# GpSimd's scaling of the residual starts after the eighth remainder of a layer norm, and the rotary table's load goes ahead of it

## The reference, cut to what matters

```python
xp = _layer_norm(ALPHA * xp + yp, ln1_g[l], ln1_b[l])     # after the mixer
xp = _layer_norm(ALPHA * xp + fp, ln2_g[l], ln2_b[l])     # after the ConvFFN
# _layer_norm: (x - mean) * rsqrt(var + eps) * g + b
```

## Time and profile before

| | us |
|---|---|
| runs | 1981.17 median of 3 (1978.34 to 1981.82) |
| the profiled execution's own time | 1974.85 |
| its span | 1973.0 |
| PE busy | 1860.7 (94%) |
| DVE busy | 902.3 (46%) |
| ACT busy | 521.5 (26%) |
| POOL busy | 149.6 (8%) |

### The profile page before, as it was taken

One profiled execution on the slowest core, in us unless ns is written; L12 is line 12 of the kernel. 1 busy time (PEld: TensorE's weight loads), 2 busy tenths in 40 slices (PEclk: granted clock), 3 DMA queues, 4 the chain that ended last, 5 costly groups with the idle time before them and its releaser, 6 DMA issues.

```text
span 1973.0 us, 35556 instructions
## 1 busy us (share of the span) xinstructions
PE 1860.7 (94%) x13514; PEld 1615.0 (82%) x13514; DVE 902.3 (46%) x1442; ACT 521.5 (26%) x734; POOL 149.6 (8%) x119
## 2 busy tenths in 40 slices
PE   8897999997999999997999998998998799999996
PEld 8894555486999999996949948957966799999996
DVE  3635443436555255535245246236237655335544
ACT  3322222213222122214222222222222422222223
POOL 0200000001000000004111210300300200000000
PEclk9998999998999999999999999999999999999999
DMA  5437888711222222221323323234324123222221
GB/s 188 165 131 242 268 282 270 258 43 43 79 92 95 76 86 91 99 76 54 136 93 119 105 110 131 80 121 144 89 98 160 47 89 99 89 75 86 97 98 45
DMA packets 83912, 234.16 MB, mean 119 GB/s; under 512 B 9617, under 2 KB 9778, under 8 KB 83490
## 3 DMA queue, kind: packets, MB, share of 16 engines
q1 hardware_dynamic: 83138, 228.19, 35.1%
q0 software_dynamic: 736, 5.48, 0.8%
HBM read 209.84 MB, written 23.80 MB: 118 GB/s over the span
## 4 chain that ended last, share of the span: by engine, by line
PE 83%; DVE 5%; issue 2%; ACT 2%; DMA 1%; DVEq 0%; SPq 0%; ACTq 0%
PE banks L1169 62%; PE banks L1246 5%; PE banks L1445 2%; PE banks L1439 2%; PE banks L1359 2%; PE banks L1431 1%; PE banks L1277 1%; PE banks L1216 1%; PE banks L1268 1%; PE banks L1287 1%; PE banks L1419 1%; DVE x_lo L942 1%; DVE y L921 1%; DMA kv<-in_vc 1%; PE banks L1280 1%
## 5 line engine op out<-in xcount | busy, mean ns | idle before, releaser
L1169 PE MATMUL banks<-x_hi,w_hi 128*128 128x272 f32 x2624 | 548.9, 291 | 44.5 <-DVE x_lo L942 30.7
L1169 PE MATMUL banks<-x_hi,w_lo 128*128 128x272 f32 x2624 | 546.0, 290 | 0.0
L1169 PE MATMUL banks<-x_lo,w_hi 128*128 128x272 f32 x2624 | 544.3, 289 | 0.0
L620 DVE TENSOR_TENSOR w_lo<-w_raw,w_hi 128x1024 fp32r<-128x1024 f32 (+2 forms) x228 | 287.4, 1260 | 515.5 <-ACT w_hi L423 515.3
L423 ACT ACTIVATE w_hi<-w_raw 128x1024 fp32r<-128x1024 f32 (+2 forms) x228 | 238.4, 1046 | 1024.6 <-PE banks L1169 989.3
L1169 PEld LDWEIGHTS banks<-x_hi,w_hi 128*128 128x128 f32 x2624 | 415.6, 190 | 49.9 <-issue 28.4
L1169 PEld LDWEIGHTS banks<-x_lo,w_hi 128*128 128x128 f32 x2624 | 415.9, 190 | 0.0
L1169 PEld LDWEIGHTS banks<-x_hi,w_lo 128*128 128x128 f32 x2624 | 412.7, 190 | 0.0
L1169 PE MATMUL banks<-act_hi,w_lo 128*128 128x272 f32 x704 | 145.2, 287 | 0.0
L1169 PE MATMUL banks<-act_lo,w_hi 128*128 128x272 f32 x704 | 145.1, 287 | 0.0
L1169 PE MATMUL banks<-act_hi,w_hi 128*128 128x272 f32 x704 | 145.0, 287 | 0.0
(11 more groups left out here) (221 smaller groups left out, 1770.4 us busy)
## 6 DMA issues: line engine op xcount, KB each, us to landing
w_raw<-in_w_up SPq DMA_DIRECT2D x88, 512.0 KB, 3.5
kv<-in_kc SPq DMA_DIRECT2D x128, 256.0 KB, 4.3
kv<-in_vc SPq DMA_DIRECT2D x128, 256.0 KB, 3.8
w_raw<-in_w_rin SPq DMA_DIRECT2D x48, 512.0 KB, 3.5
w_raw<-in_w_dn SPq DMA_DIRECT2D x32, 704.0 KB, 4.1
s<-in_s SPq DMA_DIRECT2D x32, 512.0 KB, 7.4
out_ret_s<-s SPq DMA_DIRECT2D x32, 512.0 KB, 2.6
w_raw<-in_w_in_ab SPq DMA_DIRECT2D x20, 512.0 KB, 3.6
```

The lines of the kernel that those rows point to most:

```text
L620: V.tensor_tensor(w_lo[:, j, 0:k * P], w_raw[:, j, 0:k * P], w_hi[:, j, 0:k * P].bitcast(F32), ALU.subtract).then_inc(lo_ready, 1)
L1169: last = mm(B[:, 2 * j + half, 0:HN], a[:, j, w], x[:, kt, half * HN:(half + 1) * HN], start=kt == 0 and n == 0, stop=kt == k - 1 and n == 2)
```

## The change

In scale_residual GpSimd waits once for all eight remainders of the norm, and then issues its eight instructions without a wait between them. The load of the rotary table is issued as soon as norm 1's eighth remainder is there, ahead of the eight scalings; the memset of qm stays behind them.

```diff
             def scale_residual(n):
+                pool.wait_ge(ln_done, n * KD + KD)
                 for m in range(KD):
-
-                    pool.wait_ge(ln_done, n * KD + m + 1)
                     nc.gpsimd.tensor_scalar(y[:, m, :], y[:, m, :], lnp[:, n, 1, m:m + 1], ALPHA, ALU.add, ALU.mult)\
                         .then_inc(y_scaled, 1)
 
             scale_residual(0)
 
+            pool.wait_ge(ln_done, KD + KD)
+            pool.dma_start(rope[:, :, :], A["rope"]).then_inc(rope_in, 16)
             pool.wait_ge(y_scaled, 1 + KD)
             scale_residual(1)
-            pool.wait_ge(y_scaled, 1 + 2 * KD)
-            pool.dma_start(rope[:, :, :], A["rope"]).then_inc(rope_in, 16)
             nc.gpsimd.memset(qm[:, :, :, :], 0.0).then_inc(zeroed, 1)
             pool.wait_ge(rope_in, 16)
```

## The result

The changed kernel took 1967.25 us in the median of four executions (1964.35 to 1968.72), before took 1979.76 on the same occasion (1977.19 to 1981.82): ratio 0.9939, interval 0.9924 to 0.9954, which is 9 to 15 us faster. The forecast was 1975.0 in 1971.0 to 1980.5, a gain of 6.2. The profiled execution of the changed kernel has a span of 1965.4 us, 7.6 less than the one of before.

The account below looks back on a forecast made before the run. The prediction took TensorE to be bound by VectorE's x_lo in each norm's first tile, held by GpSimd. Norms 0, 1 and 2 gain 2.6 + 1.0 + 2.6 = 6.2 us; 1981.17 - 6.2 = 1975.0, range 1971.0 to 1980.5.

Parts of the forecast that it names:

- What bounds the kernel: First tile of each norm: TensorE waits for VectorE's x_lo, 30.7 us in 18 waits, held by GpSimd's scalings.
- The gain of a norm, 2.6 us: First tile of each norm: VectorE loses six delays, so TensorE takes the last slice 2.6 us earlier.
- The cost in norm 1, 1.6 us: Behind norm 1: w_lo of tile 2 stands behind the scaling, TensorE waits 1.6 us, norm 1 keeps 1.0 us.
- The cost in norms 0 and 2: Tile 2 behind these norms: scalings delay w_lo by up to 0.46 us, hidden because TensorE needs it later.
- The rope load: GpSimd's queue in norm 1: issued about 4 us earlier, nothing as an own term; its issue costs 0.57 us.
- The sum: Whole kernel: 2.6 + 1.0 + 2.6 = 6.2 us faster, 1975.0 us from the median 1981.17; chance 0.62.
- rival (a): TensorE's clock behind norm 0: the low stretch may not come, 1.5 us more gain, 1973.5; chance 0.13 in this sense.
- (b): Scalings behind the norms: 1.19 us each but VectorE gets in between; 2.3 us faster, 1978.9, or 1980.7 at 1.41; chance 0.13.
- (c): First tile of the norms: x_lo is held by something that stays, not GpSimd; 1982.6 us; chance 0.07.
- (d): Behind all three norms: queued scalings keep VectorE out, 1.41 us each; 9.6 us slower, 1990.8; chance 0.05.
- one resource used in turns: In each norm: VectorE's scale holds GpSimd's instruction until it ends, which then holds x_lo for about 0.46 us.

Follow-up runs that it names:

- e8: The kernel before with GpSimd's 24 scalings of norms 0, 1 and 2 left out; 10.1 us faster than before, ratio 0.9952.
- e3: The changed kernel with only norm 1 gathered, rope load ahead of its scaling, norms 0 and 2 as before; 1.4 us faster than before, ratio 0.9992.
- e12: The changed kernel with VectorE's two waits moved from the retention's head to where qm is written, run again; 9.2 us faster than before, ratio 0.9957.
- e16: Like e12, but GpSimd's scaling behind norm 1 begins only when the third tile's w_lo is done; 11.0 us faster than before, ratio 0.9942.

## Why the prediction was wrong, point by point

**What bounds the kernel.** Right: the largest wait of TensorE was the one that moved, 30.7 to 23.0 us. GpSimd as the one that held x_lo was right too, by e8 and by the lengths.

**The gain of a norm, 2.6 us.** Right in every norm: in norm 1 the last slice of the first tile comes 2.57 us sooner after the first one, and the last x_lo waits 0.19 us for ScalarE, as worked out. The executions agree within their errors: 3.5 and 2.8 for norms 0 and 2 alone.

**The cost in norm 1, 1.6 us.** 1.95 in the trace. The eight scalings were 5.58 us (5.6 forecast) and the memset as forecast; GpSimd began 0.31 us behind the last x_lo instead of 0.1, and TensorE 0.3 us behind w_lo instead of 0.06. Norm 1 kept 0.6 us, not 1.0. What the prediction left out is that time won or lost here shifts the four heads behind it: removing the stall won 2.0 us up to the end of the first head and lost 1.6 of it by norm 2.

**The cost in norms 0 and 2.** Hidden, as forecast: w_lo took 0.55 us longer (0.46 forecast), and nobody waited.

**The rope load.** Nothing could be told from it; e3 has it and is worth what its step says.

**The sum.** This is where it failed. The steps sum to 5.7 us in the trace against 6.2, and the kernel gained 9 to 12.5. The missing 4 to 5 us go with the clock, which the prediction had as rival (a), with 1.5 us and a chance of 0.13, and only behind the first tile of a norm. Mis-sized is that term: the excess measures 3.6 to 5.4 us in the two repeats, with 1.7 to 3.1 thousandths of mean clock. Of its places the first tile's end is only one; the sums of norm 1 and the heads of the retention are others. The prediction took one slow stretch in one trace as the whole of what the clock could do, while before's executions, spread over 3.5 us then and over 12 later, already said that its time hangs on something which one trace doesn't show. The profiled execution of before, 1974.85, was among the quickest of its kind, so its trace had less of the slow clock than most: from norm 1's first tile to norm 2's it took 638.9 us, where the five other traces with norms 0 and 1 as before took 640.4 to 643.1.

**The rivals.** (b) is excluded by the 0.70 us steps, and (c) by e8. (d) did not happen in the changed kernel, but its mechanism, a GpSimd queue that keeps VectorE out for its whole length, does exist (e12); at 0.70 us an instruction it cost 0.8 us behind norm 1 in e12, not the 9.6 worked out for three norms at 1.41. I had called it "one resource used in turns", and that was too much to read from a stretch in which GpSimd never had two instructions ready but once. The top of the range, put at "all of (b)", is 0.2 us short of (b)'s own 1980.7; nothing hangs on that.

## What to carry to other kernels

Work on GpSimd that shares a buffer loop with VectorE can cost VectorE time even when GpSimd is 8% busy: compare the same instruction's length in places where GpSimd runs and where it doesn't, and put the GpSimd work where VectorE waits for somebody else. Look who waits for the delayed work: here one norm's gain went into a new wait. Waiting later for the scaling and starting it behind w_lo (e16) removes that from the trace, but most of the time is lost again to the lower clock in the heads that follow: take the times up to a common mark far behind an edit, too, and not only around it. Where executions of one kernel differ by more than the steps that you count, compare mean clocks over many executions before you believe a sum made from one trace.

## What the runs showed of the hardware

- A GpSimd tensor_scalar of 128x544 takes 0.70 us in a row of eight with VectorE idle (5.58 us) and holds a VectorE instruction with two SBUF inputs for 0.46 us of that. The earlier one of 128x4352 needed 11.26 us, twice as much an element, for an instruction with one operation instead of two.
- GpSimd's eight queued instructions let VectorE's w_lo in at once or after up to 0.6 us in 21 of the 22 cases in the traces (it took 1.22 to 1.80 us) and kept it out for 4.1 us in one (5.34). The Trainium skill, SBUF — State Buffer, "Who interferes with whom", says that issue order decides who is blocked, for the whole instruction. The trace has both outcomes in one kernel, and in the second the block lasts over several instructions, not one.
- Small VectorE instructions are hit as well: behind norm 0 of the changed kernel a copy of 128x2 took 0.61 us beside 0.16 before.
- An execution's time and its mean granted clock go together: 1.1 to 1.7 us for 0.001 within before's own executions, and 1.4 to 1.8 between kernels.
- The same instructions from the end of the retention's first head to norm 2 took 504.9 to 507.9 us in 18 traces. TensorE was busy at the lower level for 15.8 us between 1025 and 1520 us in the shortest (before) and for 20.9 in the longest (e3); half the difference is 2.6 of the 3.0 us.
